# Two-layer hybrid trunk on one Trainium2 core: dense products from split fp32r operands to plain fp32, weights through a ring of four slots, programs unrolled

## The chip, the core and the metric

The kernel runs on one core of one Trainium2 chip. Its engines each run a program of their own: TensorE (PE; its weight loads are listed as PEld), VectorE (DVE), ScalarE (ACT), GpSimd (POOL) and SyncE (SP), which issues most DMAs here. They meet through semaphores. SBUF is the on-chip memory of 128 partitions, PSUM the eight banks that TensorE writes to. The metric is the device time of one execution in microseconds, the median of several runs.

## What is computed

512 tokens of width 1024 get 16 meta tokens in front (528 rows) and pass through two layers. Cut to what matters:

```python
h = concat([meta, x])                                   # (528, 1024)
# layer 0
proj = h @ w_in_ab                                      # 1024 -> 2048: u, q, k, v
a = s5_mixer(u, ...)                                    # diagonal state space, gelu, y * sigmoid(y @ w_glu + b_glu)
b = stick_breaking_attention(q, k, v)                   # 8 heads of 64
h = layer_norm(ALPHA * h + concat([a, b]) @ w_out_ab)
hid = square(relu(h @ mlp_w_up[0] + mlp_b_up[0]))       # 1024 -> 4096
h = layer_norm(ALPHA * h + hid @ mlp_w_down[0] + mlp_b_down[0])
# layer 1
q, f_pre, i_in, g = split(h @ w_in_c, 4)                # 1024 -> 4096
h = layer_norm(ALPHA * h + hgrn2_mixer(q, f_pre, i_in, g) @ w_out_c)   # 8 heads, chunks of 64 rows
h = the same MLP and layer norm with the weights of layer 1
return h[16:]
```

All inputs and the output are float32. The products with weight matrices, called dense here, are nearly all of the arithmetic: 97 MB of weights, each read once.

## The kernel before

**Layout.** Activations lie transposed: `h[P, KC, L]` holds 8 chunks of 128 features by 528 rows. A dense output tile is 128 output features by 528 rows, in two PSUM banks of 264 columns each (`dense(t)`, two such pairs, used in turn). v of layer 0 and i of layer 1 are token-major: a tile is 128 rows by 256 output columns (`run_tok`).

**Plan.** `_plan` lists the dense stages in order with their slots of weights (1 MB each, 128 x 2048 floats) and tiles: uqk 6 slots, v 2, glu 1, out_ab 4, then up00, down00, up01, down01 with 8 each, i, f, g, q, out_c with 4 each, and the second MLP like the first. 97 slots in all. A slot holds 16 blocks of 128 x 128. An MLP runs in two halves of 2048 hidden units, so `h` takes two sums from the down products.

**Split products.** A value in fp32 is split into a high part in fp32r and the rest. A product of a weight block with a chunk is three fp32r matmuls for each half of the columns (`prods`, L539, L541, L543): high with high, high weight with low activation, low weight with high activation. For a slot, SP loads `raw` (L379), ACT writes `wh = raw` as fp32r (`high`, L940), POOL writes `wl = raw - wh` (`low`, L431), and then TensorE may use it (`w_lo`). `raw`, `wh` and `wl` have two slots each; SP may load a slot once POOL has split the one two before. For activations ACT writes `hh` and DVE `hl` (L1278 at the start, L1605 after a norm, L1524 for attention outputs, L1555 for the gated S5 outputs, L1736 for the heads of layer 1), and for hidden units DVE writes `hidh` and `hidl` (L1618, L1619, L1622).

**Order.** It is written out by hand. TensorE turns x into `h` (L673, L676), then runs uqk, v, the S5 stage (L705 to L741), attention over four pairs of heads (L774 to L804), glu, out_ab, a layer norm, the MLP, a norm, i, f, g, q, a loop over the eight heads of layer 1, out_c, a norm, the MLP, a norm, and turns the result back. ACT empties PSUM tiles into `tmp` (two buffers), and DVE takes them from there (`tmp_free`). In a layer norm TensorE sums over features with plain fp32 matmuls by a constant matrix (L645, L651), and `keep_warm` adds plain fp32 matmuls of 128 columns that have no use but to keep it busy (L639). After a norm `run_after` and `first_tiles` start two tiles at once: first all products with `hh`, as ACT finishes its chunks (L1151), then those with `hl`, as DVE does (L1602, L1605).

At the start DVE's program alternates copies of turned chunks (L1266, L1267) with the subtraction of the chunk before (L1278), which waits for ACT; ACT first issues 18 small DMAs. Between uqk and v ACT's `u_rows` copies u into `uj` (L1021). In the S5 stage DVE and POOL write block matrices `bt` and `cm` (L339).

**Programs.** Most stages run in register loops (`Fori`) over pairs of slots, pairs of heads or heads, with semaphore values worked out from the loop's index (`Chain.loop`).

Of the kernel before, what the change touches and what calls it, by code (L numbers as in the profile page):

```python
# [5 lines left out]
ALU = mybir.AluOpType  # L6
ACT = mybir.ActivationFunctionType
F32 = mybir.dt.float32
F32R = mybir.dt.float32r
I32 = mybir.dt.int32  # L10

P = 128
D = 1024
# [20 lines left out]

STAGES = {}


def _plan():
    slot = tile = 0
    for name, slots, per in [  # L40
        ("uqk", 6, 2), ("v", 2, NBLK), ("glu", 1, 4), ("out_ab", 4, 2),
        ("up00", 8, 2), ("down00", 8, 1), ("up01", 8, 2), ("down01", 8, 1),
        ("i", 4, NBLK), ("f", 4, 2), ("g", 4, 2), ("q", 4, 2), ("out_c", 4, 2),
        ("up10", 8, 2), ("down10", 8, 1), ("up11", 8, 2), ("down11", 8, 1),
    ]:
        STAGES[name] = (slot, slots, tile, per)
        slot += slots
        tile += slots * per
    return slot


_plan()


def tmp_tiles(before):

    names = list(STAGES)
    return sum(STAGES[n][1] * STAGES[n][3] for n in names[:names.index(before)] if n not in ("uqk", "v", "i"))

# [5 lines left out]
class Chain:  # L65


    def __init__(self, eng, sem):
        self.eng, self.sem, self.base, self.count, self.turn = eng, sem, 0, 0, 0
# [5 lines left out]
    def settle(self):  # L75

        self.eng.wait_ge(self.sem, self.turn + (self.base + self.count))

    @contextmanager
    def loop(self, turns, per):  # L80

        self.base, self.count = self.base + self.count, 0
        with self.eng.Fori(0, turns) as i:
            self.turn = i * per
            yield i
        assert self.count == per, (self.count, per)
        self.base, self.count, self.turn = self.base + turns * per, 0, 0


def trunk(nc, x, meta, w_in_ab, s5_lam_re, s5_lam_im, s5_log_dt, s5_b_re, s5_b_im, s5_c_re, s5_c_im,  # L90
          s5_d, s5_w_glu, s5_b_glu, w_out_ab, w_in_c, hgrn_gamma, hgrn_norm_g, w_out_c,
          ln_mix_g, ln_mix_b, mlp_w_up, mlp_b_up, mlp_w_down, mlp_b_down, ln_mlp_g, ln_mlp_b, out):
    with ExitStack() as ctx:
# [8 lines left out]
        mi = ExitStack()  # L102

        btt = sb("btt", [P, 2, 4, P], F32, mi)
        kt = sb("kt", [P, 2, 4, CH, 32], F32, mi)
        bt = sb("bt", [P, 2, 4, CH, 32], F32, mi)
        b0r = sb("b0r", [P, 2, 4, CH, 32], F32, mi)
        cm = sb("cm", [P, 2, 2, 4, 5, 32], F32, mi)
        ss = sb("ss", [P, 2, 2, 4, NCH + 1], F32, mi)
        mi.close()  # L110
        hh = sb("hh", [P, KC, LPAD], F32R)
        hl = sb("hl", [P, KC, LPAD], F32R)
        raw = sb("raw", [P, 2, SLOT])
        wh = sb("wh", [P, 2, SLOT], F32R)
        wl = sb("wl", [P, 2, SLOT], F32R)
# [7 lines left out]
        uqk_scale = sb("uqk_scale", [P, 3])  # L123
# [18 lines left out]
        ew = sb("ew", [P, 5, 16], F32, m0a)  # L142
        m0x = ExitStack()
# [57 lines left out]
        hidh = sb("hidh", [P, 16, L], F32R, m2)  # L201
        hidl = sb("hidl", [P, 16, L], F32R, m2)
# [33 lines left out]
        w_in = [sem("w_in_even"), sem("w_in_odd")]  # L236
        w_hi = sem("w_hi")
        w_lo = sem("w_lo")
# [8 lines left out]
        xt_hi = sem("xt_hi")  # L247
        xt_res = sem("xt_res")
        ready = sem("ready")
        mix_hi = sem("mix_hi")  # L250
        mix_ready = sem("mix_ready")
        hid_ready = sem("hid_ready")
# [9 lines left out]
        ln_hi = sem("ln_hi")  # L262
# [26 lines left out]
        glu_out = sem("glu_out")  # L289
# [10 lines left out]
        o_hi = sem("o_hi")  # L300
# [21 lines left out]
        ho = sem("ho")  # L322
# [52 lines left out]
        def _(sp_):  # L375
            def load(i, c, src, kcs=KC):

                sp_.wait_ge(w_lo, i * 2 + (c - 1))
                sp_.dma_start(raw[:, c % 2, :].rearrange("p (k n) -> p k n", k=kcs), src).then_inc(w_in[c % 2], 16)  # L379

            def stream(name, w, cols, kcs, col0=0, skip=0):
                s0, slots, _, _ = STAGES[name]
                wv = w.rearrange("(k p) n -> p k n", p=P)
                with sp_.Fori(0, (slots - skip) // 2) as i:
                    for j in range(2):
                        load(i, s0 + skip + j, wv[:, :, bass.ds(i * (2 * cols) + (col0 + (skip + j) * cols), cols)], kcs)


            def first_slot(n):
                sp_.dma_start(raw[:, n, :].rearrange("p (k n) -> p k n", k=KC),  # L390
                              w_in_ab[0].rearrange("(k p) n -> p k n", p=P)[:, :, n * 256:(n + 1) * 256]).then_inc(w_in[n], 16)
# [4 lines left out]
            first_slot(0)  # L396
            sp_.dma_start(x_tok[:, :, D // 2:D], xv[:, :, D // 2:D]).then_inc(x_in_2, 16)
            first_slot(1)
            stream("uqk", w_in_ab[0], 256, KC, skip=2)
            stream("v", w_in_ab[0], 256, KC, col0=1536)  # L400
            s0 = STAGES["glu"][0]
            load(0, s0, s5_w_glu[0].rearrange("(k p) n -> p k n", p=P), 4)
            stream("out_ab", w_out_ab[0], 256, KC)

            def mlp(layer):
                for half in range(2):
                    stream(f"up{layer}{half}", mlp_w_up[layer], 256, KC, col0=2048 * half)
                    stream(f"down{layer}{half}", mlp_w_down[layer][2048 * half:2048 * (half + 1), :], P, 16)

            mlp(0)  # L410
            stream("i", w_in_c[0], 256, KC, col0=2 * D)
            stream("f", w_in_c[0], 256, KC, col0=D)
# [15 lines left out]
        def _(pool):  # L428
# [17 lines left out]
            def lows(name, pairs=None):  # L446
                s0, slots, _, _ = STAGES[name]
                with pool.Fori(0, pairs if pairs is not None else slots // 2) as i:
                    for j in range(2):
                        low(i * 2 + (s0 + 2 + j), (s0 + j) % 2)  # L450
# [1330 lines left out]
```

## Time and profile before

| | |
|---|---|
| median of 3 runs | 1677.95 us (1677.07 to 1678.28) |
| span of the profiled execution | 1677.4 us |
| instructions in it | 28242 |
| PE busy | 1524.7 us (91%) |
| DVE, ACT, POOL busy | 758.7, 525.3, 538.0 us |
| DMA | 107.67 MB, 64 GB/s over the span |

Busy times of PE count a matmul from its start to a modelled end, and neighbours overlap; the duration of one is not the spacing of two. Spacing is read from start times in the timeline. PEclk is the clock that was granted to TensorE, as a share of full speed (2.4 GHz; half is 1.2 GHz). In a row of a view, "[6.96 <-DVE hl L1555]" tells how long the engine was idle before it and what ended that.

### The profile page before, as it was taken

What the parts mean: (1) busy time and instruction counts of PE and PEld (TensorE: products, weight loads), DVE (VectorE), ACT (ScalarE), POOL (GpSimd) and SP (SyncE); (2) the same over time, 40 slices, a digit from 0 to 9 for tenths busy, and PEclk for the clock granted to TensorE, in tenths of its full rate; (3) what the DMA queues carried; (4) which work ended last, traced back from release to release, by engine and by line L of the source; (5) the groups of instructions that cost most, each with busy time, mean ns of one, the idle gap of its engine ahead of it and who ended that gap; (6) DMA issues with size and microseconds to landing.
All of it is one profiled execution on the core that took longest, in us unless ns stands there. A gap on an engine that the chain in (4) does not pass through costs nothing.

```text
span 1677.4 us, 28242 instructions
## 1 busy us (share of the span) xinstructions
PE 1524.7 (91%) x11290; PEld 1429.4 (85%) x11290; DVE 758.7 (45%) x1171; ACT 525.3 (31%) x776; POOL 538.0 (32%) x195
## 2 busy tenths in 40 slices
PE   4977549888999999999999999889899999999997
PEld 3977534448999999999989989888798999999997
DVE  5994994444464102431150688365627430044114
ACT  2353315554332122221232733212224221222213
POOL 2334513222333433434403334300032433434330
PEclk9988857789999999999989999987799999999999
DMA  5221000001213333233202232200021233232311
GB/s 154 95 75 51 1 1 1 0 0 50 76 51 100 85 91 100 75 101 87 88 26 76 76 100 76 76 0 0 0 75 52 75 100 94 81 100 80 96 50 50
DMA packets 142009, 107.67 MB, mean 64 GB/s; under 512 B 8096, under 2 KB 139376, under 8 KB 141952
## 3 DMA queue, kind: packets, MB, share of 16 engines
q1 hardware_dynamic: 135312, 105.98, 20.6%
q10 hardware_dynamic: 6640, 0.89, 0.4%
q8 instruction: 40, 0.66, 0.2%
q14 instruction: 17, 0.14, 0.0%
HBM read 104.77 MB, written 2.10 MB: 64 GB/s over the span
## 4 chain that ended last, share of the span: by engine, by line
PE 76%; DVE 15%; ACT 4%; issue 3%; ACTq 1%; DVEq 0%
PE pb L539 19%; PE pb L541 19%; PE pb L543 19%; PE pb L785 2%; PE pb L651 2%; PE pb L892 2%; DVE uqk L1444 2%; PE pb L607 2%; PE pb L639 2%; PE pb L608 2%; PE pb L609 2%; DVE sg L1683 1%; PE pb L804 1%; PE pb L774 1%; DVE gs L1684 1%
## 5 line engine op out<-in xcount | busy, mean ns | idle before, releaser
L431 POOL TENSOR_TENSOR wl<-raw,wh 128x2048 fp32r<-128x2048 f32 x97 | 454.0, 4681 | 853.9 <-ACT wh L940 853.9
L539 PE MATMUL pb<-hh,wh 128*128 128x264 f32 x1824 | 371.1, 286 | 17.4 <-ACT tmp L1109 7.3
L541 PE MATMUL pb<-hl,wh 128*128 128x264 f32 x1824 | 369.4, 285 | 0.0
L543 PE MATMUL pb<-hh,wl 128*128 128x264 f32 x1824 | 369.2, 284 | 0.0
L539 PEld LDWEIGHTS pb<-hh,wh 128*128 128x128 f32 x1824 | 282.4, 190 | 22.0 <-issue 8.3
L541 PEld LDWEIGHTS pb<-hl,wh 128*128 128x128 f32 x1824 | 282.5, 190 | 0.0
L543 PEld LDWEIGHTS pb<-hh,wl 128*128 128x128 f32 x1824 | 282.2, 190 | 0.0
L1569 DVE SCALAR_TENSOR_TENSOR h<-h,tmp 128x528 f32 x48 | 36.5, 761 | 395.5 <-ACT tmp L1109 395.5
L539 PE MATMUL pb<-hidh,wh 128*128 128x264 f32 x1024 | 208.9, 285 | 0.0
L541 PE MATMUL pb<-hidl,wh 128*128 128x264 f32 x1024 | 208.2, 285 | 0.0
L543 PE MATMUL pb<-hidh,wl 128*128 128x264 f32 x1024 | 207.1, 283 | 0.0
L940 ACT ACTIVATE wh<-raw 128x2048 fp32r<-128x2048 f32 x97 | 184.9, 1907 | 0.0
L543 PEld LDWEIGHTS pb<-hidh,wl 128*128 128x128 f32 x1024 | 159.3, 189 | 0.0
L541 PEld LDWEIGHTS pb<-hidl,wh 128*128 128x128 f32 x1024 | 159.2, 188 | 0.0
L539 PEld LDWEIGHTS pb<-hidh,wh 128*128 128x128 f32 x1024 | 158.1, 189 | 0.0
L1618 DVE TENSOR_TENSOR tmq<-tmp 128x528 f32<-128x528 f32 x64 | 63.9, 999 | 193.3 <-ACT tmp L1109 193.3
L1109 ACT ACTIVATE tmp<-pb,cols_a 128x528 f32<-128x528 f32 x64 | 44.7, 702 | 266.9 <-PE pb L543 251.1
L1109 ACT ACTIVATE tmp<-pb 128x528 f32<-128x528 f32 x48 | 29.3, 610 | 252.4 <-PE pb L543 242.6
L607 PE MATMUL pb<-wh,hh 128*128 128x256 f32 x224 | 65.6, 293 | 11.1 <-ACT v L1010 11.1
L639 PE MATMUL pb<-mean_w,ident 128*128 128x128 f32 x528 | 66.5, 285 | 0.0
L639 PEld LDWEIGHTS pb<-mean_w,ident 128*128 128x128 f32 x528 | 65.6, 203 | 0.3
L608 PE MATMUL pb<-wl,hh 128*128 128x256 f32 x224 | 65.1, 291 | 0.0
(342 smaller groups left out, 1904.7 us busy)
## 6 DMA issues: line engine op xcount, KB each, us to landing
raw<-in_mlp_w_up SPq DMA_DIRECT2D x32, 1024.0 KB, 5.4
raw<-in_mlp_w_down SPq DMA_DIRECT2D x32, 1024.0 KB, 6.0
raw<-in_w_in_c SPq DMA_DIRECT2D x16, 1024.0 KB, 5.4
raw<-in_w_in_ab SPq DMA_DIRECT2D x8, 1024.0 KB, 5.3
raw<-in_w_out_ab SPq DMA_DIRECT2D x4, 1024.0 KB, 5.1
raw<-in_w_out_c SPq DMA_DIRECT2D x4, 1024.0 KB, 5.2
x_tok<-in_x SPq DMA_DIRECT2D x2, 1024.0 KB, 8.7
out_h<-o_tok SPq DMA_DIRECT2D x4, 512.0 KB, 3.1
```

The lines of the kernel that those rows point to most:

```text
L431: pool.tensor_tensor(wl[:, par, :], raw[:, par, :], wh[:, par, :].bitcast(F32), ALU.subtract).then_inc(w_lo, 1)
L539: pe.matmul(o[:, b, :], lh, rh[:, kc, b * LH:(b + 1) * LH], start=first, stop=False)
L541: pe.matmul(o[:, b, :], lh, rl[:, kc, b * LH:(b + 1) * LH], start=False, stop=False)
L543: mm = pe.matmul(o[:, b, :], ll, rh[:, kc, b * LH:(b + 1) * LH], start=False, stop=last)
L607: pe.matmul(o, hh[:, kc, a:a + P], wh[:, par, w], start=kc == 0, stop=False)
L608: pe.matmul(o, hh[:, kc, a:a + P], wl[:, par, w], start=False, stop=False)
L609: mm = pe.matmul(o, hl[:, kc, a:a + P], wh[:, par, w], start=False, stop=kc == KC - 1)
L639: pe.matmul(pb[:, bank, 0:P], ident[:, :], mean_w[:, :], start=True, stop=True)
L940: act.activation(wh[:, c % 2, :], raw[:, c % 2, :], ACT.Copy).then_inc(w_hi, 1)
L1109: return act.activation(halves(tmp[:, par, :]), o, func, **more)
L1569: STT(hm, hm, scale, tmp[:, (t0 + t) % 2, :], ALU.mult, ALU.add).then_inc(tmp_free, 1)
L1618: me.step(TT(a, r, r, ALU.mult))
```

## The change

1. The dense products are plain fp32 matmuls on `h`, `mx`, `uqk`, `hid` and the weights as they land. `hh`, `hl`, `raw`, `wh`, `wl`, `hidh`, `hidl` and all instructions that write them go; mixer outputs are written into a new buffer `mx[P, KC, L]`. The attention outputs are copied there by ACT alone.
2. Weights come through `ring`, four slots. SP loads slot c once TensorE is done with slot c - 4. TensorE waits for the DMA itself.
3. All 32 chunks of hidden units stay on chip (`hid[P, 32, L]`): one up stage of 16 slots and one down stage of 16, in which a tile sums over 32 chunks from two slots. `h` takes one sum per MLP, and DVE squares each hidden tile once.
4. After a norm ACT writes `h` itself and TensorE's first two tiles follow it chunk by chunk; in stage i only the first tile does.
5. All register loops are written out, on each engine.
6. ACT's `take_o` waits for `mix_ready` before it overwrites `total`. The last token tile of v has 16 rows.

The core of the diff:

```diff
-            def load(i, c, src, kcs=KC):
-                sp_.wait_ge(w_lo, i * 2 + (c - 1))
-                sp_.dma_start(raw[:, c % 2, :].rearrange("p (k n) -> p k n", k=kcs), src).then_inc(w_in[c % 2], 16)
+            def free(c):
+                for name, (s0, slots, t0, tiles) in STAGES.items():
+                    if s0 <= c < s0 + slots:
+                        if name in ("down0", "down1") and (c - s0) % 2 == 0:
+                            sp_.wait_ge(slot_half, 8 * int(name[-1]) + (c - s0) // 2 + 1)
+                        else:
+                            sp_.wait_ge(tile_done, t0 + tiles * (c - s0 + 1) // slots)
+            def load(c, src, kcs=KC):
+                if c >= RING:
+                    free(c - RING)
+                sp_.dma_start(ring[:, c % RING, :].rearrange("p (k n) -> p k n", k=kcs), src).then_inc(w_in[c % RING], 16)
...
-            def prods(o, par, w0, w1, rh, rl, kc, first, last):
-                lh, ll = wh[:, par, w0:w1], wl[:, par, w0:w1]
+            def prods(o, c, w0, moving, first, last):
                 for b in range(2):
-                    pe.matmul(o[:, b, :], lh, rh[:, kc, b * LH:(b + 1) * LH], start=first, stop=False)
-                for b in range(2):
-                    pe.matmul(o[:, b, :], lh, rl[:, kc, b * LH:(b + 1) * LH], start=False, stop=False)
-                for b in range(2):
-                    mm = pe.matmul(o[:, b, :], ll, rh[:, kc, b * LH:(b + 1) * LH], start=False, stop=last)
+                    mm = pe.matmul(o[:, b, :], ring[:, c % RING, w0:w0 + P], moving[:, b * LH:(b + 1) * LH],
+                                   start=first, stop=last)
                 return mm
...
+            def run_down(layer):
+                name = f"down{layer}"
+                s0, slots, t0, tiles = STAGES[name]
+                freed = 2 + tmp_before(f"up{layer}")
+                for m in range(tiles):
+                    pe.wait_ge(evac, t0 + m + 1)
+                    for half in range(2):
+                        c = s0 + 2 * m + half
+                        arrived(c)
+                        for kc in range(16):
+                            if m == 0:
+                                pe.wait_ge(tmp_free, freed + 16 * half + kc + 1)
+                            mm = prods(dense(t0 + m), c, kc * P, hid[:, 16 * half + kc, :],
+                                       half == 0 and kc == 0, half == 1 and kc == 15)
+                        mm.then_inc(tile_done if half else slot_half, 1)
...
-            run("out_ab", KC, 256, hh, hl, (mix_ready, 0), order=[4, 5, 6, 7, 0, 1, 2, 3])
+            run("out_ab", lambda kc: mx[:, kc, :], lambda n: (o_evac, 16 + FREE) if n < 4 else (mix_ready, n - 3),
+                order=[4, 5, 6, 7, 0, 1, 2, 3])
...
-                        act.activation(hh[:, m, 0:L], h[:, m, :], ACT.Identity, bias=b, scale=g).then_inc(ln_hi, 1)
+                        act.activation(h[:, m, :], h[:, m, :], ACT.Identity, bias=b, scale=g).then_inc(ready, 1)
...
                 act.wait_ge(o_done, i + 1 + FREE)
+                act.wait_ge(mix_ready, 4 + i)
...
-                        me.step(TT(a, r, r, ALU.mult))
-                        TT(hidh[:, m, :].squeeze(1), r, r, ALU.mult).then_inc(tmp_free, 1)
-                        me.settle()
-                        dve.wait_ge(tmp_free, i * turn + (used[0] + t + 3))
-                        TT(hidl[:, m, :].squeeze(1), a, hidh[:, m, :].squeeze(1).bitcast(F32),
-                           ALU.subtract).then_inc(hid_ready, 1)
+                    TT(hid[:, t, :], r, r, ALU.mult).then_inc(tmp_free, 1)
```

## Rows read from the trace of the kernel before

**Rows 1.** Page, part 4: chain that ended last, share of the span by line

```profile
PE pb L539 19%; PE pb L541 19%; PE pb L543 19%; PE pb L785 2%; PE pb L651 2%; PE pb L892 2%; DVE uqk L1444 2%; PE pb L607 2%; PE pb L639 2%; PE pb L608 2%; PE pb L609 2%; DVE sg L1683 1%; PE pb L804 1%; PE pb L774 1%; DVE gs L1684 1%
```

**Rows 2.** Windows view: length, busy PE, PEld, DVE, ACT, POOL, PEclk, DMA, GB/s

```profile
0.00:33.20 33.20, 10.76 (x42) 7.44 (x43) 14.38 (x26) 8.17 (x11) 6.96 (x12) 1.00 0.67 173
33.20:104.20 71.00, 71.00 (x576) 71.00 (x576) 66.66 (x160) 21.66 (x25) 28.54 (x6) 1.00 0.29 93
104.20:147.20 43.00, 32.15 (x251) 31.75 (x249) 21.07 (x28) 21.72 (x45) 9.93 (x2) 0.88 0.16 54
147.20:243.00 95.80, 44.73 (x264) 41.60 (x264) 90.89 (x130) 28.68 (x64) 38.67 (x35) 0.71 0.04 11
243.00:373.60 130.60, 116.08 (x328) 56.34 (x328) 59.97 (x189) 72.52 (x180) 36.51 (x37) 0.78 0.00 0
373.60:440.40 66.80, 59.84 (x482) 59.62 (x482) 24.55 (x29) 22.04 (x29) 18.28 (x4) 0.95 0.19 61
440.40:459.20 18.80, 16.54 (x111) 14.85 (x109) 10.98 (x17) 9.69 (x14) 4.55 (x1) 1.00 0.20 66
459.20:832.70 373.50, 372.33 (x3074) 371.65 (x3075) 106.87 (x141) 92.96 (x85) 145.23 (x31) 1.00 0.29 87
851.50:918.40 66.90, 64.03 (x480) 61.00 (x481) 13.66 (x29) 17.54 (x29) 13.86 (x3) 0.92 0.15 48
918.40:1066.00 147.60, 140.07 (x1154) 138.68 (x1152) 101.13 (x80) 65.42 (x84) 57.71 (x15) 1.00 0.26 85
1066.00:1205.50 139.50, 121.00 (x731) 107.20 (x729) 84.89 (x123) 30.24 (x72) 14.37 (x15) 0.80 0.03 9
1205.50:1254.60 49.10, 49.06 (x386) 49.09 (x387) 15.97 (x21) 11.24 (x13) 13.76 (x3) 0.94 0.20 62
```

**Rows 3.** Lines view by form, TensorE: the group of L539 with hh

```profile
L539 PE MATMUL pb<-hh,wh 128*128 128x264 f32 x1824 | 371.1, 286 | 17.4 <-ACT tmp L1109 7.3 <-DVE hl L1555 7.0 <-POOL wl L431 1.8
```

**Rows 4.** Timeline, TensorE, in an up stage: start, length, line, count

```profile
473.13 0.40 PE L541 MATMUL pb<-hl,wh 128*128 128x264 f32 x2
473.37 0.40 PE L543 MATMUL pb<-hh,wl 128*128 128x264 f32 x2
473.61 0.40 PE L539 MATMUL pb<-hh,wh 128*128 128x264 f32 x2
```

**Rows 5.** Timeline, TensorE, in layer norms

```profile
440.40 2.84 PE L639 MATMUL pb<-mean_w,ident 128*128 128x128 f32 x24
443.07 1.10 PE L645 MATMUL pb<-total,mean_w 128*128 128x264 f32 x4
...
1653.86 1.94 PE L651 MATMUL pb<-tmp,mean_w 128*128 128x264 f32 x8
1655.64 1.94 PE L651 MATMUL pb<-tmq,mean_w 128*128 128x264 f32 x8
```

**Rows 6.** Timeline of SP, ACT, DVE and TensorE around waits; a DMA's landing

```profile
2.28 0.59 SPq L397 DMA_DIRECT2D x_tok<-in_x  x1
DMA to landing us min/median/max: 11.4/11.4/11.4
19.21 1.18 ACT L985 ACTIVATE hh<-h 128x528 fp32r<-128x528 f32 x2 [17.12 <-issue]
...
107.06 14.29 ACT L1021 ACTIVATE tmp<-uqk 32x132 f32<-32x132 f32 x32
...
150.15 5.81 DVE L339 TENSOR_TENSOR cm<-wc,group 128x640 f32<-128x640 f32 x2
...
395.25 0.81 PE L539 MATMUL pb<-hh,wh 128*128 128x264 f32 x2 [6.96 <-DVE hl L1555]
...
850.59 5.87 ACT L1151 ACTIVATE hh<-h,cols_a 128x528 fp32r<-128x528 f32 x8 [3.08 <-DVE h L1596]
```

**Rows 7.** Page, parts 5 and 6: the splits of weights, and a slot's landing

```profile
L431 POOL TENSOR_TENSOR wl<-raw,wh 128x2048 fp32r<-128x2048 f32 x97 | 454.0, 4681 | 853.9 <-ACT wh L940 853.9
L940 ACT ACTIVATE wh<-raw 128x2048 fp32r<-128x2048 f32 x97 | 184.9, 1907 | 0.0
...
raw<-in_mlp_w_down SPq DMA_DIRECT2D x32, 1024.0 KB, 6.0
```

## What the change was predicted to do

> **What bounds the kernel now.** I read the page first: the chain that ended last runs mostly over TensorE, and its three longest lines are L539, L541 and L543, the three partial products of a dense step, 19% each [rows 1]. Then I cut the span into stages and read each one's busy times [rows 2]. Two kinds of stage show. In the dense ones (33.2 to 104.2 us, each MLP of 373.5 us, 918.4 to 1066, 1205.5 to 1254.6) TensorE is busy nearly all the time and DVE, ACT and POOL are far below it. In the others (the start, 147.2 to 243, attention, the head loop from 1066) TensorE waits or runs code that the change leaves as it is. So the question is what a dense step costs on TensorE before and after.
>
> **Counts.** By the plan of stages, 91 slots hold 32 products of 264 columns each, 2912 in all (1824 of them are the L539 row of [rows 3]), and 6 slots hold 40 token-major products of 256 columns, 240. Each is now three fp32r matmuls.
>
> **Price of a product before.** From 473.13 to 473.61 us four matmuls start [rows 4], so 120 ns each and 360 ns a product. One MLP has 1024 products, 368.6 us of its 373.5 [rows 2]. The mean duration of 286 ns in [rows 3] is latency, not spacing; multiplied by the count it would be more than twice the span of these stages.
>
> **Price after.** Plain fp32 is in the trace already, in the layer norms. L651 has two matmuls of 264 columns per chunk, and two chunks (four matmuls) appear as eight records: a plain fp32 matmul is two records. Eight of them take 1653.86 to 1655.64, so 222.5 ns a record [rows 5] and 445 ns a product. Is TensorE waiting for squares there? No: an ACT pass over a chunk takes 0.6 us [rows 6], these four records 0.89. And 24 records of 128 columns in L639, which wait for nothing, take 443.07 - 440.40 = 2.67 us, 111 ns each [rows 5]: the time follows the columns. Do new weights cost more than the norm's constant ones? In [rows 4] weights change with each matmul at 120 ns, so a load fits well under a record of 222.5. I take 445 ns, and 432 ns for 256 columns (445 x 256/264). Bounds for a record: 220 (I allow 2.5 for waiting in the norm's spacing) to 231 (an fp32r record of 264 columns takes 120, 8.75 more than half of 222.5; if that excess comes with every change of weights, it is added). The records are 2 x 3152 = 6304, so a ns is 6.3 us and the bounds are -16 and +54 us.
>
> So a product gets 24% dearer although the matmuls in the program fall to a third. What goes away beside it, ACT's 97 copies of 1.9 us and POOL's 97 subtractions of 4.7 us [rows 7] and DVE's low parts, lies beside TensorE in the dense stages, and is worth something only where TensorE waited for it.
>
> **Stage by stage** (lengths before from [rows 2]).
> 1. Start, 33.2: TensorE is busy for 10.8 us only, since DVE's copies of the transposes stand behind its hl subtraction, that behind ACT's hh copy, and ACT issues DMAs until 19.2 [rows 6]. This goes. Late next is the second half of x, issued at 2.28 and landed 11.4 us later, at 13.7 [rows 6]. Four more chunks of transposes (10.8/8 = 1.3 each) and some 1.8 us of DVE's copies and row transposes end at 20.8. -12.4.
> 2. uqk, 71.0: 576 matmuls make 69.1; 1.9 is over and stays. 192 x 0.445 + 1.9 = 87.3. +16.3. Each of the six slots now lasts 14.2 us, and a 1 MB slot lands in 6 [rows 7], so the ring is never empty.
> 3. 104.2 to 147.2: ACT splits a slot, then copies u for 14.3 us [rows 6], and TensorE waits with two v tiles done. The split goes (-1.9), the first two tiles still vanish in the wait, eight tiles of eight products add 64 x 0.072 = 4.6. +2.7.
> 4. S5, 95.8: DVE's two cm products take 5.8 us beside POOL's split [rows 6] and alone under 2, so up to 4 could go; but TensorE has 16 records of L734 to do meanwhile. I take -1 (0 to -4).
> 5. Attention, 130.6: DVE's low parts of the outputs go; ACT's chain goes on beside them. I take -1 (0 to -5).
> 6. glu and out_ab, 66.8: TensorE waits 7.0 us for the last hl subtraction [rows 6], then runs at half clock for a while. Now the gate of glu's last tile (five operations of some 0.7 us) ends in 4 us, while TensorE does the four chunks from attention (3.6 us) and three earlier ones (2.7). The wait goes. 160 x 0.445 = 71.2. +4.4.
> 7. Each MLP, 373.5: 455.7 and 1.4 over (4.9 now, of which the wait for hl goes; ACT feeds a chunk in 5.87/8 = 0.73 us [rows 6], TensorE takes 1.78 for it). +83.6, twice +167.2. A square of DVE per up tile (under 1 us) hides under 7.1.
> 8. i, 66.9: the first tile follows ACT, 7 x 0.73 + 0.43 = 5.6; 19 tiles of 3.46 are 65.7; 0.4 for an evacuation. +4.8.
> 9. f, g, q, 147.6: 24 x 7.12 = 170.9 and 1 for changeovers. +24.3. The chains of ACT and DVE are covered: with the splits in them a tile lasts 147.6/24 = 6.15 now.
> 10. Head loop, 139.5: the hh and hl steps that go stand beside the state products. ACT's new wait for mix_ready holds back its four activations of an output, for which TensorE waits, but DVE's product that it asks for is made while TensorE still works on that output. 0 (-2 to +1).
> 11. out_c, 49.1: 128 x 0.445 = 57.0, and the 3.0 over 384 x 0.120 stays. +10.9.
>
> The norms and the output stay. SP's waits for a free slot stand ahead of later loads only. Sum: -12.4 + 16.3 + 2.7 - 1 - 1 + 4.4 + 167.2 + 4.8 + 24.3 + 10.9 = +216.2. The profiled span is 1677.4, 0.55 below the median of 1677.95: 1677.4 + 216.2 + 0.55 = 1894.
>
> **Unrolling.** A loop's turn could have cost time; but an MLP, with 16 turns in it, is 4.9 us over its matmuls [rows 2], so it is a few tenths of a us per turn at most, already counted. The Trainium skill (Runtime: NRT & Kernel Launch, Instruction fetch mechanics) says that a taken branch to a page not held forces a fetch and a stall, which speaks for unrolling. The trace shows no such stall of size; by that rule the sum would be at most 7 us lower.
>
> **Rivals.**
> A. Every plain record with new weights carries fp32r's excess: 231 ns. +54, so 1948. For it: fp32r does exceed its columns. Against: L639's records, with a load before each, follow the columns at 111. 0.11.
> B. A long plain fp32 stream does not hold the granted clock. In the head loop and attention, all plain fp32, it averages 0.80 and 0.78 [rows 2]; at 0.80 the 1399 us of products take 1749, about 2244. Against: TensorE has holes there, and a norm holds 1.00. 0.04.
> C. The unrolled program arrives late. At a hole of 0.9 us (a pair of products) per slot, 97 x 0.9 = 87: 1981. Against: a loop's body is straight code too and runs without holes. 0.05.
> D. Not slower: in a dense stream the passes of successive plain matmuls overlap, and the norm's 222.5 ns is no price for it. The place is every dense stage; it decides from 222.5 - 216/6.3 = 188 ns a record down. At 131 ns it gives 577 less, 1317, and some 20 back where f and g are bound by their chains: 1340. Against: 24 records of L639 in a row without a wait. 0.04.
> The Trainium skill (TensorE: Matmul & The Clock Gate, Back-to-back issue gap) gives 131 ns as sustained spacing at 512 columns, which is D's figure. The trace differs: 222.5 ns for a record of 264 columns in two passes.
>
> **How the numbers follow.** Forecast 0.76, with 1868 to 1915 as its own range (record from 220, stages within 10 us), A 0.11, C 0.05, B 0.04, D 0.04. The range takes in A and the bounds of a record, 1868 to 1950, and leaves out B, C and D. Under 0.2% is what this kernel's measurement can't tell from no change. Only D can end there or below: faster 0.03, same 0.01, slower 0.96.
>
> **What will show it.** Records of the dense line 222 or 223 ns apart at a granted clock of 1.00; an MLP of 457 us; the first product at 21 us; no hole between glu and out_ab; 7.1 us per tile in f, g and q; POOL nearly idle. The forecast is wrong if the spacing is another, if the clock falls in a dense stage, or if holes come at even distances in it.

## The result, and the profile after

The changed kernel takes 1893.62 us at the median of four runs (1887.17 to 1903.32), the kernel before, in the same comparison, 1677.87. The ratio is 1.1287 with a 95% interval of 1.126 to 1.1315: slower by 216 us. The profiled run is one of the quicker ones, 1888.08 us with a span of 1886.3.

First the page of the changed kernel: the busy times (us, share of the span, instructions), the granted clock in 40 slices, the chain that ended last by engine and by line, and the costliest group.

```profile
PE 1771.6 (94%) x8138; PEld 1474.8 (78%) x8138; DVE 506.8 (27%) x943; ACT 329.3 (17%) x643; POOL 73.8 (4%) x87
PEclk9998777899999999999999999878999999999999
...
PE 87%; DVE 7%; ACT 3%; ACTq 1%; issue 1%; DVEq 0%
PE pb L479 69%; PE pb L548 5%; PE pb L802 2%; PE pb L697 2%; PE pb L556 2%; PE pb L568 2%; DVE uqk L1294 1%; PE pb L716 1%; PE pb L686 1%; DVE d L1514 1%; DVE d L1510 1%; PE pb L768 1%; PE pb L701 1%; ACT tmp L907 1%; ACTq L872 1%
...
L479 PE MATMUL pb<-h,ring 128*128 128x264 f32 x3200 | 715.6, 387 | 5.5 <-ACTq L874 3.9
```

One line, L479, is now 69% of the chain, where three lines shared it before [rows 1], and POOL is down to 4%. The mean of 387 ns in the last row is latency, as the 286 ns of [rows 3] was. The spacing is read from the stages. The windows of the changed kernel (start and end, length, then busy time and count for PE, PEld, DVE, ACT and POOL, granted clock, DMA share, GB/s):

```profile
24.40:111.90 87.50, 87.50 (x384) 74.36 (x385) 44.79 (x167) 10.16 (x19) 0.00 (x0) 1.00 0.21 64
113.00:157.40 44.40, 36.71 (x161) 28.06 (x160) 11.06 (x12) 17.18 (x41) 0.00 (x0) 0.92 0.15 48
157.40:252.10 94.70, 43.50 (x267) 40.62 (x265) 87.35 (x132) 27.00 (x64) 33.70 (x35) 0.74 0.03 12
252.10:377.50 125.40, 112.63 (x329) 55.22 (x329) 52.34 (x174) 72.17 (x180) 27.77 (x28) 0.80 0.00 1
377.50:448.60 71.10, 71.10 (x321) 60.73 (x321) 16.03 (x23) 12.65 (x21) 0.00 (x0) 1.00 0.20 60
467.60:923.30 455.70, 455.70 (x2048) 388.86 (x2049) 36.31 (x53) 32.11 (x46) 0.00 (x0) 1.00 0.25 72
942.30:1013.30 71.00, 70.88 (x320) 60.23 (x321) 4.86 (x13) 12.10 (x26) 0.29 (x1) 1.00 0.15 45
1013.40:1184.00 170.60, 170.60 (x769) 145.65 (x767) 67.34 (x80) 45.01 (x72) 1.28 (x2) 1.00 0.24 74
1184.00:1322.10 138.10, 124.36 (x731) 110.37 (x729) 76.72 (x116) 24.43 (x64) 9.44 (x14) 0.80 0.03 8
1322.10:1380.80 58.70, 58.70 (x256) 49.85 (x257) 14.01 (x20) 5.47 (x9) 0.00 (x0) 0.97 0.19 54
1399.80:1855.60 455.80, 455.80 (x2048) 388.96 (x2049) 36.30 (x53) 32.13 (x46) 0.00 (x0) 1.00 0.23 65
```

These answer to the stages of [rows 2], in the same order, without the start and the norm; the last is the second MLP. The sixth row is the plainest: an MLP of 2048 records takes 455.7 us, so 222.5 ns a record, two records and 445 ns a product, at a granted clock of 1.00 and without a hole. In f, g and q (the eighth row) TensorE is busy from end to end as well: 170.6/24 = 7.1 us a tile. The frame shows in the fifth row, where no hole is left between glu and out_ab.

### The profile page after: what moved, and what is told of

Its sections match the earlier page's. It is cut to its first block, busy times and chain, and to the rows that moved or that the text cites. A ratio compares the mean times of both kernels' runs of the same rounds, so it can differ in the third digit from the quotient of the medians.

```text
span 1886.3 us, 18691 instructions
## 1 busy us (share of the span) xinstructions
PE 1771.6 (94%) x8138; PEld 1474.8 (78%) x8138; DVE 506.8 (27%) x943; ACT 329.3 (17%) x643; POOL 73.8 (4%) x87
## 4 chain that ended last, share of the span: by engine, by line
PE 87%; DVE 7%; ACT 3%; ACTq 1%; issue 1%; DVEq 0%
PE pb L479 69%; PE pb L548 5%; PE pb L802 2%; PE pb L697 2%; PE pb L556 2%; PE pb L568 2%; DVE uqk L1294 1%; PE pb L716 1%; PE pb L686 1%; DVE d L1514 1%; DVE d L1510 1%; PE pb L768 1%; PE pb L701 1%; ACT tmp L907 1%; ACTq L872 1%
## 5 line engine op out<-in xcount | busy, mean ns | idle before, releaser
L479 PE MATMUL pb<-h,ring 128*128 128x264 f32 x3200 | 715.6, 387 | 5.5 <-ACTq L874 3.9
L479 PEld LDWEIGHTS pb<-h,ring 128*128 128x128 f32 x3200 | 609.1, 190 | 111.3 <-issue 6.9
L479 PE MATMUL pb<-hid,ring 128*128 128x264 f32 x2048 | 456.0, 386 | 0.0
L479 PEld LDWEIGHTS pb<-hid,ring 128*128 128x128 f32 x2048 | 389.1, 190 | 66.6
L1430 DVE TENSOR_TENSOR hid<-tmp 128x528 f32<-128x528 f32 x64 | 45.3, 708 | 407.6 <-ACT tmp L995 407.6
L479 PE MATMUL pb<-mx,ring 128*128 128x264 f32 x512 | 116.2, 391 | 0.9 <-DVE sg L1520 0.9
L548 PE MATMUL pb<-ring,h 128*128 128x256 f32 (+1 forms) x480 | 108.2, 385 | 8.6 <-ACT v L897 7.7
L479 PEld LDWEIGHTS pb<-mx,ring 128*128 128x128 f32 x512 | 98.5, 193 | 19.6 <-DVE sg L1520 2.4
L548 PEld LDWEIGHTS pb<-ring,h 128*128 128x128 f32 (+1 forms) x480 | 88.4, 186 | 27.8 <-ACT v L897 8.1
L697 PE MATMUL pb<-sp,ntri 128*128 128x32 f32 (+4 forms) x80 | 38.1, 565 | 21.9 <-DVE sp L1344 21.9
```

Of the source, the lines that this page charges most:

```text
L479: mm = pe.matmul(o[:, b, :], ring[:, c % RING, w0:w0 + P], moving[:, b * LH:(b + 1) * LH], start=first, stop=last)
L548: mm = pe.matmul(pb[0:rows, 2 * (t % 2), 0:256], h[:, kc, a:a + rows], ring[:, (s0 + j) % RING, kc * 256:(kc + 1) * 256], start=kc == 0, s ...
L697: mm = pe.matmul(pb[:, u, 0:UW[u]], ntri[:, :], sp[:, n % 2, 0:UW[u]], start=False, stop=u == 0, skip_group_check=True)
L1430: TT(hid[:, t, :], r, r, ALU.mult).then_inc(tmp_free, 1)
```

## The experiments

All times are medians, each beside runs of the kernel before on the same chip (1678.4 to 1678.7 in these comparisons).

**Price and frame apart.** The change is a dearer product and a frame around it: no splits, a four-slot ring, fewer waits, no loops. Two kernels take one of them each. The first pays the price in the kernel before:

```diff
-                lh, ll = wh[:, par, w0:w1], wl[:, par, w0:w1]
+                lh = wh[:, par, w0:w1].bitcast(F32)
                 for b in range(2):
-                    pe.matmul(o[:, b, :], lh, rh[:, kc, b * LH:(b + 1) * LH], start=first, stop=False)
-                for b in range(2):
-                    pe.matmul(o[:, b, :], lh, rl[:, kc, b * LH:(b + 1) * LH], start=False, stop=False)
-                for b in range(2):
-                    mm = pe.matmul(o[:, b, :], ll, rh[:, kc, b * LH:(b + 1) * LH], start=False, stop=last)
+                    mm = pe.matmul(o[:, b, :], lh, rh[:, kc, b * LH:(b + 1) * LH].bitcast(F32), start=first, stop=last)
```

> The kernel before with one edit: each dense product is one plain fp32 matmul on the high parts, where three fp32r matmuls stood. The splits of ACT, DVE and POOL, the loops, the buffers and the waits stay. The low parts are computed and not used, so the sums lack them. Theory (the two parts of the change are a price of TensorE and a frame around it, and they add up): 2912 products dearer by 85 ns and 240 by 72 are +265 us, less what still falls into TensorE's waits at the v stage, glu and the starts of the MLPs (some 20), so about 1919; the span of an MLP is then 456 to 461 and a record of the dense line 222 to 223 ns. Rival (the splits and their waits disappear behind a TensorE that takes longer, so the frame is worth next to nothing once the price is paid): within 5 us of 1894. A third outcome, under 1880, would say that the unsplit frame costs time by itself.

Measured: 1926.0 us (1925.8 to 1926.7), ratio 1.1479 (1.146 to 1.1498), 7 us over the theory's 1919: of the 265 us some 17 fell into waits, where I had allowed for more than 20. The rival's 1894 is out. The second kernel cuts the changed kernel's products to the old price (the first block of a tile stays whole):

```diff
-            def prods(o, c, w0, moving, first, last):
+            def prods(o, c, w0, moving, first, last, n=206):
+                n = LH if first else n
...
-                    mm = pe.matmul(o[:, b, :], ring[:, c % RING, w0:w0 + P], moving[:, b * LH:(b + 1) * LH],
+                    mm = pe.matmul(o[:, b, 0:n], ring[:, c % RING, w0:w0 + P], moving[:, b * LH:b * LH + n],
```

> The changed kernel with its products cut until one costs what it cost before, about 360 ns: two matmuls of 206 of the 264 columns (211 in the down projections, 205 of 256 columns in the token-major products), except for the first product of each tile, which stays whole. The sums of the left-out columns are therefore incomplete. Ring, no splits, waits and unrolled program are those of the change. Theory: what is left against the kernel before is the frame alone: about 9 us at the start, 2 in the v stage, 3 in S5, 4 in attention, 9 at glu and out_ab, 2 at each MLP, some at i and out_c, so a time of about 1625 (1615 to 1635) against 1678. Rival (in f, g and q, and in glu, the chains of ACT and DVE bound as soon as TensorE is as fast as before, since a tile's activations stay what they were): 1635 to 1650. If it lands at 1670 or above, the frame is worth nothing at the old price.

Measured: 1627.8 us (1626.8 to 1639.5), ratio 0.9702 (0.9686 to 0.9718). Four of its five runs lie between 1626.8 and 1628.6; the profiled one is the fifth, and its attention takes 137.3 us, of which more below. The windows of an MLP, first with the price alone, then with the frame alone, and of f, g and q with the frame alone:

```profile
496.10:952.10 456.00, 455.83 (x2048) 388.98 (x2049) 97.19 (x141) 92.89 (x85) 143.07 (x31) 1.00 0.25 72
```

```profile
446.40:815.30 368.90, 368.71 (x2048) 363.22 (x2049) 36.32 (x53) 32.16 (x46) 0.00 (x0) 1.00 0.31 89
893.90:1032.20 138.30, 138.30 (x769) 135.04 (x767) 67.39 (x80) 44.91 (x72) 1.77 (x2) 1.00 0.30 92
```

With the price alone POOL still subtracts for 143 us beside the MLP and ACT works 93, and the MLP is as long as after the change, 456.0 against 455.7: there the splits cost nothing once a product takes 445 ns. With the frame alone 1024 products take 368.7, 360 ns each, so the cut did hit the old price. The frame is then worth 1678.4 - 1627.8 = 50.6 us; the price alone costs 1926.0 - 1678.4 = 247.6. The two make +197, where the change measured +216.

By the medians the frame is worth only 1926.0 - 1893.6 = 32.4 us once the price is paid. But the changed kernel's runs fall into a shorter and a longer group, as is shown below, while the 1627.8 stands for the shorter runs of its kernel. Against the changed kernel's shorter runs (1887 to 1888) the frame is worth 38.6, so 12 us are to be explained and not 18. They are found in f, g and q and in the MLPs, where TensorE had short waits before: 147.6 and 373.5 us in [rows 2], 138.3 and 368.9 with the frame alone. Under the dearer products these waits are covered with or without the frame (f, g and q 170.7 us with the price alone and 170.6 after, an MLP 456.0 and 455.7). That is 9.2 us and twice 4.3. The other stages together go 5 to 6 us the other way, some 3 of them in attention, which takes 132.5 us with the price alone and 129.6 in the kernel before.

The rival of the second kernel, that the chains of ACT and DVE bind, falls: in the last row TensorE is busy all the time, and in glu with out_ab too (58.2 of 58.2 us). Only the fifth run lies in the rival's range.

**The first product.** It starts at 24.3 us, where the prediction had 20.8. The changed kernel's timeline around it (start, length, engine and line; in brackets the idle time before and what ended it):

```profile
12.17 9.37 ACTq L872 DMA_DIRECT2D cn<-in_s_c_re  x2
...
20.02 0.39 PE L595 MATMUL pb<-ident,lin_b 112*128 112x112 f32 x1
...
21.57 2.56 ACTq L872 DMA_DIRECT2D cn<-in_s_c_im  x2
...
24.32 2.98 PE L479 MATMUL pb<-h,ring 128*128 128x264 f32 x6 [3.91 <-ACTq L874]
```

TensorE is done with its transposes at 20.4 and then waits 3.9 us for L874, ACT's increment of evac, which stands behind the DMA issues for cn.

```diff
+            act.sem_inc(evac, 2)
+            act.sem_inc(o_evac, FREE)
             for ri, src in enumerate([s5_b_re, s5_b_im]):
...
-            act.sem_inc(evac, 2)
-            act.sem_inc(o_evac, FREE)
```

> The changed kernel with two lines moved: ACT's increments of evac and o_evac, which free the accumulators for the first product, stand ahead of its two DMA issues for bb and cn instead of behind them. Theory (the first product starts at 24.3 us and not at the 20.8 of the prediction because it waits for an increment that stands behind two DMA issues on ACT): the first product starts at 20.6 (20 to 21.5), and the time falls by 3.5 us (2 to 4). Rival (something else is late next, ACT's copies of h or the landing of the first slots): the first product stays above 23, and the time moves by less than 1 us.

Measured, the row of the first product:

```profile
19.27 5.58 PE L479 MATMUL pb<-h,ring 128*128 128x264 f32 x14
```

The first product starts at 19.3, 5.0 us earlier, and the rival falls. Of the 5.0 the two lines gave 4 to 4.6: TensorE was also done with its transposes 0.9 earlier, since the second half of x landed earlier in this run, and against the next experiment's run, where it landed as early, the gain is 23.9 - 19.3 = 4.6. The median is 1889.2 (1882.6 to 1893.8; ratio 1.1248, 1.1214 to 1.1281). That is 4.4 below that of the change, but the two intervals overlap, and the profiled run was 5 us longer than the profiled run of the change: its attention had taken 137.1 us instead of 125.4. That led to the next question. With its answer the runs can be compared group by group: 1882.6 and 1885.0 against 1887 to 1888, 1893.4 and 1893.8 against 1898 to 1903. Each group lies lower, the shorter by 2 to 5 us and the longer by 5 or more.

**Where the spread comes from.** The same changed kernel, run again:

> The changed kernel once more, unchanged. Its four runs lay between 1887 and 1903 us, while the looped kernels stay within 2 or 3 us. In the profiles so far attention (from its first cumulative-sum product to glu's first product) took 125.4 us with 49.8 us of it at half the clock in the changed kernel, 137.1 with 78.4 in the one with two moved lines, 129.6 with 56.3 in the kernel before. Theory (the spread is attention's, by how much of it the granted clock is halved): if this profile's span differs by more than 3 us from 1886.3, the difference lies between 252 and 378 us, with the half-clock time there longer by about twice the difference or more; every dense stage keeps its length within 0.3 us. Rival (the unrolled program is fetched late at times): the difference lies in dense stages as holes between records.

Measured: 1898.6 us (1887.1 to 1899.4), ratio 1.1286 (1.1251 to 1.1321). Of the eight runs of the changed kernel in all, three lie between 1887 and 1888 and five between 1898 and 1903. This time the profile shows one of the longer ones (span 1897.0). Its windows of attention and of an MLP:

```profile
251.20:388.30 137.10, 126.18 (x329) 59.92 (x329) 52.54 (x174) 72.49 (x180) 27.78 (x28) 0.71 0.00 1
478.40:934.10 455.70, 455.70 (x2048) 388.86 (x2049) 36.31 (x53) 32.15 (x46) 0.00 (x0) 1.00 0.25 72
```

Attention is 137.1 us at a mean granted clock of 0.71, where the first profile had 125.4 at 0.80, with the same records and the same work of DVE and ACT. Attention is 11.7 us longer, the two spans differ by 10.7, and the MLP is 455.7 in both. 78.4 us of attention are at half clock, where the first profile had 49.8, and TensorE's busy time grew by some 13.5 us while its waits did not grow (12.8 before, 10.9 now): it is the records that take longer. So the theory holds, though uqk, 0.4 us longer, moved a little more than the 0.3 that it allowed. Late program code, which would have shown as holes in the dense stages, does not come into it.

**What writing out the loops does.** First all loops of the kernel before, then only attention's, then all but attention's. The edit is of one kind:

```diff
-            with me.loop(NPAIR, 22) as i:
+            for i in range(NPAIR):
```

> The kernel before with all its loops written out, nothing else. Theory (a turn of a loop costs TensorE nothing in a dense stage, and the writing out has no part in what the change brings): 1675 to 1678, 0 to 3 us less than before. Rival (branches cost a fetch each time, and the writing out is worth time): 1665 or less. A second rival (a longer straight program is fetched late): over 1681, with holes at even distances in TensorE's rows.

Measured: 1672.1 us (1667.1 to 1682.2, ten runs), ratio 0.9965 (0.9947 to 0.9983), so 6 us less. Both the theory (0 to 3) and the rivals (1665 or less, or over 1681) missed it. So attention was told apart from the rest.

> The kernel before with only attention's three loops over the head pairs (on TensorE, ACT and DVE) written out. So far: all loops written out gave 1672 us at the median, with runs between 1667 and 1682, where the looped kernel's runs stay within 1676.5 to 1683. Theory (the writing out changes how attention falls on the stretches of half clock, so the spread comes from here; the gain does not): median 1675 to 1679, runs over 8 us or more. Rival (the spread belongs to a written-out program as such, wherever the loops were): runs within 4 us, median within 2 us of 1678.5.

> The kernel before with every loop written out except attention's three. Theory (the gain of writing out lies in f, g and q, where the chains of ACT and DVE end the wait of TensorE and their loop turns count, 4.3 us, and about 1 us each at the start and in out_c; the spread lies in attention): median 1671 to 1673, runs within 4 us of each other. Rival (the spread belongs to the written-out program as such): runs spread over 8 us or more here too.

Measured: with attention alone 1679.7 us (1678.2 to 1688.6; eight of eleven runs between 1678.2 and 1680.2, three between 1686.8 and 1688.6), ratio 1.0017 (1.0002 to 1.0032). With all but attention 1672.4 (1671.4 to 1673.9), ratio 0.996 (0.9947 to 0.9974). The first median is 0.7 above its theory's range; the spreads are as the theories said. So the two effects come apart: the gain of 6.3 us comes without touching attention, and the runs that are 9 us longer come with attention written out. The window of f, g and q with all but attention written out, and what TensorE waited for there (us in total, times, longest):

```profile
916.80:1061.60 144.80, 139.37 (x1154) 138.41 (x1152) 102.19 (x80) 65.56 (x84) 58.18 (x15) 1.00 0.28 88
...
PE pb L539 <- ACT tmp L1109: 4.3, 3, 1.8
PE pb L539 <- POOL wl L431: 1.1, 2, 0.6
```

It is 144.8 us against 147.6 in [rows 2], where the same two waits of the kernel before read:

```profile
PE pb L539 <- ACT tmp L1109: 5.7, 3, 2.5
PE pb L539 <- POOL wl L431: 1.8, 2, 0.9
```

Both shrink, by 2.1 us together, and that is most of the 2.8; the theory had 4.3 for this place. Stages i and out_c are shorter by 0.9 and 1.1 us. Which instruction of a loop's turn costs this has no row of its own.

**The frame without the price.** Those parts of the frame that looked worth time were then put on the three fp32r matmuls. It is not the whole frame: the splits, the two slots each of `raw`, `wh` and `wl` and the MLPs in two halves stay. All loops are written out, and the order of work on SP, ACT and DVE is changed. Parts of the edit:

```diff
-            u_rows(0)
-            u_rows(1)
-            run("v", to_tok(v0))
...
+            for t in range(slots * per):
+                if t < 8:
+                    u_row(t // 4, t % 4)
+                act.wait_ge(tile_done, t0 + t + 1)
+                v_tile(0, t, dense(t0 + t), (t0 + t) % 2).then_inc(evac, 1)
+                if t % per == per - 1:
+                    high(0, s0 + t // per + 2)
...
-            high(0, s0 + 2)
-
             for m in range(4):
                 act.wait_ge(glu_out, m + 1)
                 act.activation(hh[:, m, 0:L], uqk[:, m, :], ACT.Copy).then_inc(mix_hi, 1)
+            high(0, s0 + 2)
...
+            for kc in range(KC):
+                b = 2 * (kc % 2)
+                dve.wait_ge(xt_done, kc + 1)
+                dve.tensor_copy(h[:, kc, 0:400], pb[:, b, 0:400]).then_inc(xt_res, 1)
+                dve.tensor_copy(h[:, kc, 400:L], pb[:, b + 1, 0:P]).then_inc(xt_res, 1)
...
```

> The kernel before (three fp32r matmuls a product, all splits) with what the experiments say is worth time in the change's frame: all loops written out; the DMA issues for bb and cn moved from ACT to SP; DVE copies all transposes of the first h before its hl subtractions; ACT's second split at the start waits for the last of those; ACT copies u between the v tiles instead of ahead of them; ACT's split of out_ab's second slot moved behind glu's four hh copies. Theory (the gain of the frame is separate from the plain products): 6 us for the loops, 8 at the start, 10 in the v stage, 4 at glu: about 1650 (1642 to 1660) against 1678. Rival (POOL's split and DVE's subtractions hold each other up, so that the start and glu gain nothing): 1660 to 1672.

Measured: 1639.4 us (1638.6 to 1648.9), ratio 0.9777 (0.9752 to 0.9803): 39 us less than before, better than the theory by 11 and outside its range on the good side. Its windows of uqk, v, and glu with out_ab:

```profile
20.00:92.60 72.60, 71.19 (x576) 71.01 (x576) 67.21 (x163) 21.95 (x25) 28.30 (x6) 1.00 0.32 100
93.60:122.30 28.70, 28.70 (x242) 28.70 (x240) 27.18 (x28) 20.97 (x44) 9.25 (x2) 1.00 0.23 74
345.00:404.40 59.40, 57.79 (x480) 57.58 (x480) 23.87 (x29) 22.05 (x29) 18.32 (x4) 1.00 0.22 68
```

The first product starts at 20.0 instead of 33.2, 13 us where 8 were expected. Part of that comes back in uqk, 1.6 us longer. The v stage is 28.7 us against 41.6 from its first to its last record before, and TensorE never stops in it. glu with out_ab is 59.4 against 66.8 [rows 2]. The rival named something real, which the new order avoids. In the kernel before, one of DVE's hl subtractions at the start fell beside POOL's split of a slot:

```profile
25.21 4.50 POOL L431 TENSOR_TENSOR wl<-raw,wh 128x2048 fp32r<-128x2048 f32 x1 [21.90 <-ACT wh L940]
...
25.75 4.52 DVE L1278 TENSOR_TENSOR hl<-h,hh 128x528 fp32r<-128x528 f32 x1 [0.52 <-ACT hh L985]
```

It took 4.52 us, where the other seven at the start take 0.70. The one between glu and out_ab for which TensorE waited 7.0 us [rows 6] took 4.58, beside the next split of POOL (390.13 to 394.63 us). With the new order the twelve subtractions of these two places take 0.70 us each. This is the kernel to keep of those run, with one question left: one of its five runs lies 9 us above the others. So attention's loops were put back:

> The kernel that had the frame's gains on three fp32r matmuls (1639.4 us at the median, runs 1638.5 to 1648.9), with attention's three loops put back. Theory (the spread belongs to attention written out, its gain to the other stages): median 1637 to 1641, runs within 4 us. Rival (the looped attention was steady only because it began where it did; begun 28 us earlier it can fall on the half clock as well): runs spread over 8 us or more, or a median off 1639 by more than 4.

Measured: 1641.9 us (1640.8 to 1642.2), ratio 0.9778 (0.9764 to 0.9791). The runs lie within 1.4 us; the median is 0.9 above the theory's range. The rival's spread does not show. Five runs alone do not rule it out: had one run in five been a long one, as in the kernel before this, five short ones in a row would still come in a third of cases. But the looped attention was also steady over four runs with the price alone, where it begins at 264 us, and over the fifty runs of the kernel before, where it begins at 244; here it begins at 219. Against a rival that needs one moment of starting, that speaks clearly, though it is no proof. Against four of the five runs of the kernel with all loops written out, 1638.6 to 1640.1, the looped attention costs about 2.5 us.

**What a short record costs.** The cut of the second experiment, taken to 64 columns:

```diff
-            def prods(o, c, w0, moving, first, last, n=206):
+            def prods(o, c, w0, moving, first, last, n=64):
```

> The changed kernel with every product but the first of each tile cut to 64 columns; the sums of the other columns are left incomplete. It asks what a plain fp32 record costs when its moving side is short, and what bounds the frame once TensorE doesn't. If the time goes by columns alone, a record of 64 columns takes 54 us/1000 (0.843 ns a column, as at 264 columns; 206 columns took 174.7, so 0.848); if a load of new weights bounds it, some 100 to 120 ns (128 columns in the norms' keep-alive records took 111). In the MLPs the loads of 1 MB slots, which landed in about 6 us each, should bound next: 32 slots of 5 to 6 us, so an MLP of 160 to 200 us instead of 456, and a time of 1000 to 1150 us in all.

Measured: 1352.3 us (one run), some 200 us over the highest expectation. The windows of an MLP and of stage i:

```profile
415.50:662.40 246.90, 246.46 (x2048) 241.17 (x2048) 36.24 (x53) 32.03 (x46) 0.00 (x0) 1.00 0.46 133
681.30:759.60 78.30, 76.60 (x320) 71.99 (x321) 4.89 (x13) 12.15 (x26) 0.29 (x1) 0.53 0.14 41
```

In the MLP 160 records are whole (in each of the 32 up tiles and eight down tiles the first block, four records) and take 160 x 0.2225 = 35.6 us. The 1888 short ones share 211.3: 112 ns each, where columns alone would give 54. At 206 and 211 columns the same sum gives (368.9 - 35.6)/1888 = 176.5, where columns alone give 176. So between 264 and 206 columns the time follows the columns, and at 64 it has a floor of 112, about what 128 columns take in [rows 5]. The window fits the guess that a load of new weights sets the floor (PEld is busy 241 of 247 us), but no run varied the load alone, so that is argued and not shown. The loads of the slots, expected to bound, did not: 133 GB/s at a DMA share of 0.46, with TensorE busy 246.5 of 246.9 us.

The second row is the other reason for the miss. Stage i takes 78.3 us, 7 more than in the changed kernel (71.0), although its records are mostly short, because the granted clock averages 0.53 there. An estimate from the rows above: 280 short records at twice 112 ns and 40 whole ones of 256 columns at twice 216 ns would make 80.

## Why the prediction was right, point by point

- **The price of a product** carried the forecast and held: 222.5 ns a record, two records a matmul, 445 ns a product, with new weights each time. Rival A (231 ns) would have made an MLP 473 us; it is 455.7. Rival D (the passes overlap) would have needed 188 ns or less. The 24 records of L639 and the eight of L651 [rows 5] were enough to fix both. The kernel with the price alone confirms it: +247.6 measured, where 265 had been counted and some 17 fell into waits.
- **The clock** stays at 1.00 in uqk, in glu with out_ab, in both MLPs, in i and in f, g and q (v has 0.92, with waits in it, out_c 0.97), so rival B falls for this change. It was not absurd: with short records the clock did fall in a dense stage, as the last experiment shows.
- **Program fetch** (rival C): no holes in the dense stages. The Trainium skill (Runtime: NRT & Kernel Launch, Instruction fetch mechanics) says that a taken branch to a page not held forces a fetch and a stall. By that rule the prediction allowed up to 7 us for unrolling; writing out all loops of the kernel before but attention's brought 6.3, but no row names a fetch, so the agreement is one of size only.
- **MLPs**: +83.6 each predicted; +82.6 each measured (each stage here from its first record to the next stage's first, an MLP from the last record of the norm before it). **uqk** +16.3, measured +16.7; **v** +2.7, measured +2.9; **glu and out_ab** +4.4, measured +4.5, and the wait for an hl subtraction is gone as said (it was the first of four, not the last, and long because POOL worked beside it); **i** +4.8, measured +4.2; **f, g, q** +24.3, measured +23.0; **out_c** +10.9, measured +10.0.
- **The start** is the step that failed: -12.4 predicted, -8.9 measured (24.3 us). The step said that ACT's DMA issues no longer stand in anyone's way once the hh copies go. It overlooked that the increment of evac, for which the first product waits, stands behind the same issues; and these got longer, 9.37 and 2.56 us for cn where the kernel before had 5.23 and 1.09. SP issues four 1 MB slots at the start now instead of two, the last of them until 13.2 us; that their transfers hold up ACT's issues fits this but was not tested. Moving two lines brought the first product to 19.3. The step's own estimate, 20.8, was then 1.5 us too careful, most of it because the second half of x landed 1.2 us before the 13.7 it had assumed.
- **Attention** was put at -1 (0 to -5). In the first profile it is -4.2, within that; in the second +7.6, outside it, without a change in its work. The step counted only work and had no term for the clock, so it failed for the longer runs. The forecast of 1894 lies between the two groups of runs (1887 to 1888 and 1898 to 1903), and that the median of the first four runs is 1893.6 is luck: over all eight it is 1898.5. The fair comparison is stage by stage: the first profile's span is 208.9 us longer where the forecast had +216.2. What is off is the start, 3.5 over, and on the other side attention (3.2), S5 (1.6), the head loop (1.4), f, g and q (1.3), the MLPs (1.0 each) and out_c (0.9).
- **S5** -2.6, **head loop** -1.4, both within their ranges; norms and the output moved by half a us in all. In S5 DVE's two cm products take 1.6 us now instead of 5.8, as the prediction said.
- **The frame**: the prediction did not price it as a whole. The experiments do: 50.6 us at the old price and 38.6 at the new one, both by the shorter runs.

## What to carry to other kernels

Price the inner operation from a place of the old trace where the same operation already stands in a row without waits, and multiply by records: counted so, the price was +265 us, in a run of its own +248, and the savings beside the busiest engine gave back 39 to 51 of them. When a change mixes a dearer operation with a leaner frame, run the two apart; here a part of the frame, on the old matmuls, gave a kernel 2.2% faster (ratio 0.9778, 0.9764 to 0.9791, with attention looped), while the change as a whole was 12.9% slower. When a wait is said to go, list everything that its engine still does ahead of the next signal, bare semaphore increments behind DMA issues among it.

## What the runs showed of the hardware beyond that

**Attention's length goes with the granted clock, and one program can come in more than one length.** Over the twelve profiles of this study it took 125.4 us with 49.8 us of it at half clock, 128.2 with 53.0, 128.4 with 56.7, 129.6 four times (twice with 56.3, with 59.6 and 59.7), 132.5 with 63.5, 137.1 and 137.2 with 78.4, 137.3 with 79.3, and 140.4 with 85.4. In between TensorE waits for DVE and ACT at every step, so it is in and out of work throughout. The kernel before, with looped attention, stayed within 1676.5 and 1683.5 us in all its runs. Why a written-out attention falls into the longer form in some runs is open: no run varied the moment at which attention begins and nothing else.

**The clock can halve in a stage in which TensorE has no long waits.** In stage i of the kernel with 64-column products TensorE is busy 76.6 of 78.3 us at a mean granted clock of 0.53, where the whole products of the changed kernel hold 1.00 in the same stage (70.88 of 71.00). That is one profile of one run.

**Short plain fp32 records have a floor** of 112 ns at full clock (64 columns; 0.843 ns a column at 264), so by this estimate cutting columns below about 112/0.843 = 133 would gain nothing here.

**A DMA issue can hold its engine for microseconds.** ACT's issues for cn took 9.37 us for two, then 2.56 us for two more; everything behind them on ACT waits, an increment of a semaphore included.

**A POOL subtraction can hold up one of DVE for its whole length.** A DVE subtraction over 128 x 528 took 0.70 us alone and 4.5 us beside a POOL subtraction of 4.5 us, while POOL's took no longer than elsewhere (4.7 in the mean [rows 7]); in the kernel before this stood once ahead of the first product and once between glu and out_ab.
